# Two-layer hybrid decoder step: order of VectorE's state work in the heads, and the place of the state sums

## The reference

```python
def _layer(x, c, pos, state, ...):
    h = _rmsnorm(x, g_norm) * (1.0 + scale) + shift          # adaLN from c
    cols = jnp.split(h @ w_in, ...)
    o_hg, hg_s_new = _hgrn2_chunked(...)                      # 4 heads
    o_ml, ml_c_new, ml_n_new, ml_m_new = _mlstm_chunked(...)  # 6 heads
    o_rt, rt_s_new = _retention_chunked(...)                  # 6 heads
    o = concatenate([head_norm(o_hg), head_norm(o_ml) + skip * q_c, head_norm(o_rt)]) * silu(z)
    y = x + gate * (o @ w_out)

# every kind has, per chunk, a state sum and an output; mLSTM also a normalizer n:
s_new = decay * s + einsum('bhsk,bhsv->bhkv', k * state_decay, v)
n_new = decay_c * n + einsum('bhs,bhsk->bhk', w_s, k)
h = num / maximum(abs(den), exp(-m_t))     # den = inter_w * (n . q) + row sums of the scores
```

## Time and profile before

| | us |
|---|---|
| median of 3 runs | 2336.93 (2336.76 to 2337.56) |
| the profiled execution's own time | 2337.24 |
| its span, first to last instruction | 2335.6 |
| TensorE busy | 2275.7 |
| VectorE busy | 1286.6 |
| ScalarE busy | 738.6 |
| GpSimd busy | 938.5 |

### The profile page before, as it was taken

The page is one execution under the profiler, slowest core; times in us unless marked ns, Lnnn a source line. Parts: engine busy times, 40 slices in busy tenths (PEclk is TensorE's granted clock), DMA queues, the critical chain, the costliest instruction groups (busy, mean ns, idle before and its releaser), DMA issues.

```text
span 2335.6 us, 50231 instructions
## 1 busy us (share of the span) xinstructions
PE 2275.7 (97%) x21347; PEld 2164.6 (93%) x21347; DVE 1286.6 (55%) x2506; ACT 738.6 (32%) x1175; POOL 938.5 (40%) x668
## 2 busy tenths in 40 slices
PE   4899999999999999999999999999999999999998
PEld 3799999999999999998879999999999999999998
DVE  6346666677776343442137566667777753335444
ACT  2143322333333333421124333333333333334111
POOL 3043333333344343554333333333333443346552
PEclk9999999999999999999999999999999999999999
DMA  9952223544443333266775222254443323323332
GB/s 399 374 184 93 92 93 99 160 164 161 161 171 98 115 99 114 97 223 239 268 267 197 84 94 93 84 168 155 163 162 102 107 98 122 116 84 110 116 117 105
DMA packets 153648, 347.21 MB, mean 149 GB/s; under 512 B 14817, under 2 KB 85409, under 8 KB 127545
## 3 DMA queue, kind: packets, MB, share of 16 engines
q1 hardware_dynamic: 153424, 344.01, 42.8%
HBM read 312.07 MB, written 32.09 MB: 147 GB/s over the span
## 4 chain that ended last, share of the span: by engine, by line
PE 89%; DVE 4%; DMA 2%; DVEq 1%; ACT 1%; issue 1%; POOL 1%; SPq 0%; ACTq 0%; POOLq 0%
PE pj L685 72%; PE mx L691 3%; PE mx L1028 2%; PE mx L1054 2%; DMA rows<-in_ada_first 1%; PE mx L778 1%; PE mx L1042 1%; PE mx L744 1%; PE pj L1150 1%; PE mx L1006 1%; PE mx L1056 1%; DVE t L1501 1%; PE mx L1046 1%; POOL wlo L653 1%; DMA spare_piece<-in_ada_first 1%
## 5 line engine op out<-in xcount | busy, mean ns | idle before, releaser
L685 PE MATMUL pj<-hh,whi 128*128 128x260 f32 x4928 | 1417.7, 288 | 5.7 <-DVE hl L1501 5.2
L653 POOL TENSOR_TENSOR wlo<-raw,whi 128x512 fp32r<-128x512 f32 x632 | 894.6, 1447 | 1307.6 <-ACT whi L1229 1307.6
L685 PE MATMUL pj<-hl,whi 128*128 128x260 f32 x4928 | 1392.3, 283 | 0.0
L685 PE MATMUL pj<-hh,wlo 128*128 128x260 f32 x4928 | 1389.9, 282 | 0.0
L685 PEld LDWEIGHTS pj<-hh,whi 128*128 128x128 f32 x4928 | 928.0, 188 | 52.0 <-issue 45.4
L685 PEld LDWEIGHTS pj<-hl,whi 128*128 128x128 f32 x4928 | 928.4, 188 | 0.0
L685 PEld LDWEIGHTS pj<-hh,wlo 128*128 128x128 f32 x4928 | 927.9, 188 | 0.0
L1229 ACT ACTIVATE whi<-raw 128x2048 fp32r<-128x2048 f32 x158 | 302.8, 1916 | 257.4 <-PE pj L685 186.7
L1229 ACT ACTIVATE xv<-pj 128x260 f32<-128x260 f32 x188 | 64.8, 383 | 386.5 <-PE pj L685 386.2
L1501 DVE SCALAR_TENSOR_TENSOR o<-pj,mod,t 128x260 f32<-128x260 f32 (+1 forms) x56 | 24.6, 480 | 229.9 <-PE pj L685 214.3
L1229 ACT ACTIVATE t<-t 128x520 f32<-128x520 f32 (+1 forms) x126 | 79.2, 629 | 178.9 <-DVEq L1761 129.6
(11 more groups left out here) (289 smaller groups left out, 2329.8 us busy)
## 6 DMA issues: line engine op xcount, KB each, us to landing
raw<-in_w_tiles SPq DMA_DIRECT2D x128, 1024.0 KB, 4.9
raw<-in_wo_tiles SPq DMA_DIRECT2D x32, 1024.0 KB, 5.2
lev<-in_w_ada SPq DMA_DIRECT2D x90, 256.0 KB, 4.4
rows<-in_ada_first SPq DMA_DIRECT2D x22, 1024.0 KB, 20.7
lev<-in_w_ada SPq DMA_DIRECT2D x39, 512.0 KB, 5.7
out<-ss SPq DMA_DIRECT2D x32, 512.0 KB
xv<-in_w_ada SPq DMA_DIRECT2D x25, 512.0 KB, 5.8
y_kept<-o SPq DMA_DIRECT2D x2, 4160.0 KB, 18.0
```

The lines of the kernel that those rows point to most:

```text
L653: last = e.tensor_tensor((wlo_third if t == 2 else wlo[:, par, :])[:, cs], w[:, cs], high_of(t)[:, cs].bitcast(F32), ALU.subtract)
L685: last = e.matmul(pj[:, 2 * par + b, 0:HALF], w[:, par, kb * P:(kb + 1) * P], x[:, kb, b * HALF:(b + 1) * HALF], start=(kb == 0 and m == 0 ...
```

## The change

It changes the order on two engines.

1. On VectorE, the inputs of the samples' state sums (`sw`, the ones, the block copy `big`) come first, then the scaling of `ss`, then `q_pairs`.
2. The normalizer update of the mLSTM heads comes behind the addition to `ss`. Its scratch is a part of `t3` in place of `sw`.
3. `states_u` moves an eighth of a tile up in all heads but head 0 of layer 0. In the two short mLSTM heads `ml_os` moves up an eighth too.
4. In head 15 two of VectorE's four low parts go behind the addition to `ss`.

```diff
@@ hooks_of
-                                   {0: (level_scores((6,)),), 2: (rows,), 5: (states_u,), 7: (outputs,)})
+                                   {0: (level_scores((6,)),), 2: (rows,), 4: (states_u,), 7: (outputs,)})
                         if kind == "ml" and session_of(h, 0) >= SESSIONS[l]:
-                            return ({}, {}, {2: (scores, rows), 6: (states_u,)}), {0: (outputs,), 4: (ml_os,), 7: (back,)}
+                            return ({}, {}, {2: (scores, rows), 5: (states_u,)}), {0: (outputs,), 3: (ml_os,), 7: (back,)}
                         if kind == "ml":
-                            return ({}, {}, {1: (scores, rows), 5: (states_u,), 7: (outputs,)}), {3: (ml_os,), 7: (back,)}
+                            return ({}, {}, {1: (scores, rows), 4: (states_u,), 7: (outputs,)}), {3: (ml_os,), 7: (back,)}
...
-                        return ({}, {}, {1: (scores, rows), 5: (states_u,), 7: (outputs,)}), {5: (back,)}
+                        return ({}, {}, {1: (scores, rows), 4: (states_u,), 7: (outputs,)}), {5: (back,)}
@@ VectorE
-                        e.wait_ge(state_in[g % 2], (g // 2 + 1) * 16)
-                        tt(ss, ss, bc(token_decay, 2, HD), M)
+                        def low_first(kbs):
+
+                            for kb in kbs:
+                                e.wait_ge(o_hi, l * KB + kb + 1)
+                                tt(hl[:, kb, :], o[:, kb, :], hh[:, kb, :].bitcast(F32), S_).then_inc(o_lo_first, 1)
+
                         e.wait_ge(as_["sr"], g + 1)
                         if kind == "ml":
-
-                            ts(sw[0:GR], sr[0:GR, 1, :], gs[0:GR, i, 1:2], None, M)
-                            e.drain()
-                            e.wait_ge(nrow_in[g % 2], 32 * same_parity(g))
-                            stt(nr[0:GR], nr[0:GR], gs[0:GR, i, 0:1], sw[0:GR], M, A_)
-                            e.drain().then_inc(vs["nrow"], 1)
-                            e.tensor_tensor_reduce(out=t3[0:GR, 0:HD], in0=nr[0:GR], in1=sr[0:GR, 0, :], scale=1.0, scalar=0.0,
-                                                   op0=M, op1=A_, accum_out=sm[0:GR, 63:64])
                             ts(sw[0:GR], sr[0:GR, 2, :], gs[0:GR, i, 1:2], None, M)
                             e.memset(vt[:, :, HD:HD + 1], 1.0)
                             blocks(sr[0:GR, 1, :], big[0:GR, 0:256])
-                            blocks(sr[0:GR, 0, :], q_pairs[0:GR, :])
                         else:
                             blocks(sr[0:GR, 2, :], big[0:GR, 0:256])
                         e.drain().then_inc(vs["blk"], 1)
+                        e.wait_ge(state_in[g % 2], (g // 2 + 1) * 16)
+                        tt(ss, ss, bc(token_decay, 2, HD), M)
+                        if kind == "ml":
+                            blocks(sr[0:GR, 0, :], q_pairs[0:GR, :])
+                        e.drain()
 
                         if h + 1 == NH:
-                            for kb in range(LOW_FIRST):
-                                e.wait_ge(o_hi, l * KB + kb + 1)
-                                tt(hl[:, kb, :], o[:, kb, :], hh[:, kb, :].bitcast(F32), S_).then_inc(o_lo_first, 1)
+                            low_first(range(LOW_FIRST // 2))
...
                         tt(ss4, ss4, mx[:, 0:4, 256:512], A_)
                         e.drain().then_inc(vs["ss"], 1)
+                        if kind == "ml":
+                            kn = t3[0:GR, HD:2 * HD]
+                            ts(kn, sr[0:GR, 1, :], gs[0:GR, i, 1:2], None, M)
+                            e.drain()
+                            e.wait_ge(nrow_in[g % 2], 32 * same_parity(g))
+                            stt(nr[0:GR], nr[0:GR], gs[0:GR, i, 0:1], kn, M, A_)
+                            e.drain().then_inc(vs["nrow"], 1)
+                            e.tensor_tensor_reduce(out=t3[0:GR, 0:HD], in0=nr[0:GR], in1=sr[0:GR, 0, :], scale=1.0, scalar=0.0,
+                                                   op0=M, op1=A_, accum_out=sm[0:GR, 63:64])
+                            e.drain()
+                        if h + 1 == NH:
+                            low_first(range(LOW_FIRST // 2, LOW_FIRST))
```

## The result

| | before | after |
|---|---|---|
| median, us | 2337.01 (2336.76 to 2337.56, 4 runs) | 2323.55 (2322.17 to 2325.36, 4 runs) |
| profiled execution | 2337.24 | 2323.17 |
| its span | 2335.6 | 2321.6 |

The ratio is 0.9941, with a 95% interval of 0.9928 to 0.9953: faster by 13.5 us, or 0.58%. The forecast was 7.3 us and 2329.6, its range ended at 2328.3. The direction was right, and the gain is almost twice the forecast.

A forecast was written before the change was run, and what follows sets the result against it. TensorE, busy 97% of the span, was taken as the bound, so only removing its waits pays. Terms 2.4 + 3.3 + 2.0 = 7.7, less 0.4, gave -7.3 us: median 2329.6 us, range 2328.3 to 2333.2.

The forecast's parts named there:

- the last row: Weight-load row before the outputs hook: 11.0 us in 32 places, 3.3 already counted, 7.7 taken as the hook's fixed cost.
- The sums' waits: State-sum hook in three mLSTM heads: VectorE's inputs ready with 0.8 us to spare, so the wait goes, -2.4 us.
- The outputs' waits: Outputs hook in five heads: sums an eighth earlier remove the waits for the finished sample state, -3.3 us.
- The turn back in short heads: Heads 9 and 10 of layer 1: turn moved up an eighth removes waits of 0.89 and 1.1, -2.0 us.
- The normalizers at no cost: Normalizers behind the state addition: 1 to 1.5 us expected, covered by VectorE's wait for the outputs, costed at nothing.
- the rule quoted in the prediction: SBUF: a two-input VectorE instruction contends with a GpSimd instruction reading SBUF; whoever issues first holds the shared pair.
- HGRN2 heads: Before the state sums: only two eighths remain after the rows, 0.8 us left, no wait in eight heads.
- The layer ends: Second output tile at each layer end: TensorE about 1.1 us earlier meets GpSimd's low copy, 0.2 us taken back each.
- I take it as following: VectorE's part of the layer-end head: starts 1.15 us earlier too, so assumed to come forward to match.
- The first: Rival at layer ends: moved subtractions delay GpSimd's low copy, 1.4 us more lost at each, 2332.4; chance 0.15.
- The short heads: Rival in short mLSTM heads: VectorE, ScalarE, GpSimd chain does not come forward, 1.6 + 2.0 return, 2333.2; chance 0.10.
- The slower one: Rival in 8 HGRN2 and 12 mLSTM heads: GpSimd stretches the scaling, 0.7 us falls on TensorE each, 2343.6; chance 0.03.

The follow-up runs named there:

- the new places alone: The kernel before with all hooks at their new places and VectorE's old order kept: 2345.07 us, ratio 1.0034.

## Why the prediction was right in direction and too small

**The step that failed** is the reading of the last row: "the other 7.7 are 0.24 in each of 32 heads, which I take as the fixed cost of that hook and not as a wait: TensorE's own row has only 5". The runs put a true wait there. The reason given for it was the error: TensorE's own row has only 5 because a matmul is drawn 0.28 long where the next can start after 0.12, so an idle stretch below 0.16 stays invisible and a slightly longer one shows as next to nothing. Two readings of the trace before would have shown it: the step of 0.34 in place of 0.12 in front of the outputs, and VectorE's addition that ended 0.09 before them in a head that was supposed not to wait. An equal size in heads of three kinds looked like a constant; it was one because the same chain ran against the same two eighths in nearly all of them.

**The sum, term by term.** The heads gained 16.1 us, against 7.7 booked. The 8.4 more are 0.27 on average for the 31 heads whose sums moved, the failed step: 5.1 in the eighteen heads without a drawn wait, and 3.3 in the others. For the same reason a wait that was booked is longer than drawn: 0.39 before the outputs is a step of 0.67 in place of 0.12, a loss of 0.55. The change's own costs behind the layer ends were 1.9, where 0.4 was booked, a second and smaller miss. The 1.1 won before the first outputs and the 1.3 lost to the clock between the layers are scatter: 16.1 - 1.9 + 1.1 - 1.3 = 14.0.

- *The sums' waits, 2.4:* right. The inputs were ready with 0.8 to spare, and L1042 left the list.
- *The outputs' waits, 3.3:* right as far as it went; all five are gone.
- *The turn back in short heads, 2.0:* right in its cause, and near in size. Moving the turn alone back by an eighth costs 1.7, and two waits of 0.7 return.
- *The normalizers at no cost:* right. (The prediction counts one more drain in an mLSTM head. The diff adds two there and one in every other head; no wait in the lists above comes from them.) They take 1.2 us and end at about 1799.83 in head 9 of layer 1, 2.3 before VectorE's next work. I had put their former length down to GpSimd. The operation on `nr`, kernel before and then after:

```profile
L1501 DVE SCALAR_TENSOR_TENSOR nr<-nr,gs,sw x12: 352/1220/1226, 430.9 to 1856.5; 98x128 f32<-98x128 f32 x12
```

```profile
L1501 DVE SCALAR_TENSOR_TENSOR nr<-nr,gs,t x12: 350/352/353, 435.5 to 1852.8; 98x128 f32<-98x128 f32 x12
```

  (shortest, median and longest in ns). Beside GpSimd's low copy it took 1220, behind it 352. That an operation with two SBUF inputs and GpSimd's disturb each other is what the rule quoted in the prediction says, and the trace agrees. The scaling with one tensor input grew as well (1.31 beside GpSimd in head 9, 0.29 alone), on which that sentence says nothing. GpSimd's busy time fell too, from 938.5 to 907.0.
- *HGRN2 heads:* right, no wait before the sums. The 0.30 before the level scores of head 1 of layer 0 was not foreseen.
- *The layer ends, 0.2 each:* too small, they cost 0.8 and 1.1. The low copy cost 0.35, near enough; but "I take it as following" of VectorE's part was wrong. Its last scaling ran beside GpSimd (1.33 us in place of 0.33) and finished 26.8 us after the head's rows, against 26.9 before, while TensorE came 0.8 earlier; so the turn back waits 0.76. The experiment that puts the turn back a quarter later takes these waits away.

**The rivals.** The first, that the layer ends give it back, was partly right in its place, not in its size (1.1 at each end, not 1.4 beyond the forecast's 0.2). The short heads gave back next to nothing: one new wait of 0.17 for a low copy, in head 10 of layer 1, is all of its sign that appeared. The slower one, with the scaling last in the chain, did not occur: in the HGRN2 heads the scaling lasted 1.23 and was done 2.1 before the sums ended. In head 9 of layer 1 it lasted 2.10 and was done only 0.2 before.

**The 1.1 us up to the first outputs** are not the change's. Over the fourteen profiled executions told of here that point lay between 143.6 and 148.1. In six of them the granted clock was full from 100 to 150 us, and they came at 143.6 to 144.2, the changed kernel's two among them; in the other eight it fell somewhere between 102 and 112 us, and they came at 144.7 (the kernel before) to 148.1. In the windows of the kernel before:

```profile
103.00:106.00 3.00, 2.71 (x36) 2.23 (x37) 0.00 (x0) 0.00 (x0) 0.00 (x0) 0.50 1.03 391
106.00:109.00 3.00, 3.00 (x48) 2.66 (x48) 0.20 (x1) 0.30 (x2) 0.00 (x0) 0.96 0.92 352
```

**What stays open.** Why that fall comes in some executions and not in others no run here tells. The same kind of small wait, 3.1 us in 15 weight loads before the level scores of the HGRN2 heads (L1028), is still there after the change; whether it can be won was not tried.

## What to carry to other kernels

A small idle time that the weight loads show in every repetition is a wait until proven otherwise: compare the starts of neighbouring matmuls with their usual step, and look whether the releaser ended just before. Clearing the way of the inputs alone gained 4.2 us, moving their consumer earlier alone lost 8, and both together gained 13.5, so two such halves should not be priced apart. Where a producer shares its engine with other work, split that work and put in front only what is needed first; here half of the subtractions, moved behind the chain, was worth about 5 us. And look at what an operation does where it stands: the scaling of `ss` used to fill a wait, and put behind that wait it made the subtractions of head 15 start 1.2 us later.

## What the runs showed of the hardware

I had not expected how short a standstill can halve TensorE's clock. In these traces TensorE waited eight times for 2.2 to 2.4 us in the middle of dense work, and seven times the granted clock fell from 1.00 to 0.50, that is from 2.4 to 1.2 GHz, for 6.8 us in the heads and 3.4 at the layer ends. The fall began between 0.4 us before the wait's end and 1.3 us behind it. Before the sums it cost 3.1 us, more than the wait. No wait of 0.8 to 1.2 us was followed by one. Between 150 us and the last 30 of each span the clock fell nowhere else but between the layers. The wait of 1.85 to 1.87 at the start of layer 1 occurs in every trace, and was followed by a fall in two of fourteen. The kernels with long waits also scattered most: 2341.1 to 2350.5 for the new places alone, against 2322.1 to 2326.2 for the changed kernel.
